# A one-core decoder layer with 64 streamed experts: two extra 1 MB weight slots, TensorE bodies written out, and one weight scaling and the closing norm reordered

## What is computed

```
scores = sigmoid(t @ router_w)                     # 256 tokens, 64 experts
...                                                # top 6 experts of the top 4 groups, gates w
a = einsum('td,edf->tef', t, w1)                   # w1, w3: 64 x 1024 x 256
b = einsum('td,edf->tef', t, w3)
hid = silu(a) * b * gates
routed = einsum('tef,efd->td', hid, w2)            # w2: 64 x 256 x 1024
shared = (silu(t @ sw1) * (t @ sw3)) @ sw2
x = x + gate_f * (routed + shared)
return rms_norm(x, final_norm_g)
```

## Time and profile before

| | us |
|---|---|
| median of 3 runs | 787.99 (787.81 to 791.71) |
| the profiled execution | 788.67 |
| its span, first to last instruction | 786.9 |
| PE busy, share of the span | 729.7, 93% |
| DVE busy | 325.1, 41% |
| ACT busy | 173.5, 22% |
| POOL busy | 8.6, 1% |
| moved by DMA | 271.33 MB, mean 345 GB/s |

### The profile page before, as it was taken

How to read it: one execution, slowest core, us unless ns; L and a number is a source line. 1 busy time by engine, 2 the same in 40 slices (tenths; PEclk the granted TensorE clock), 3 DMA queues, 4 the chain that set the end, 5 groups by cost and what they waited for, 6 DMA issues and landing times.

```text
span 786.9 us, 12545 instructions
## 1 busy us (share of the span) xinstructions
PE 729.7 (93%) x5000; PEld 389.4 (49%) x5000; DVE 325.1 (41%) x810; ACT 173.5 (22%) x348; POOL 8.6 (1%) x22
## 2 busy tenths in 40 slices
PE   4699999999999998999998998999999997999894
PEld 1478888888886454333343333343434332333332
DVE  1119493855556486323333233231333322323324
ACT  3223320200000232212122122120222211212213
POOL 0200001000000000000000000000000000000000
PEclk9999999999999998999999999999999999999997
DMA  9999627695959355999999999999999999999981
GB/s 338 378 348 365 195 88 221 234 310 182 349 203 418 143 237 211 370 421 421 420 420 421 420 421 420 421 421 419 384 421 420 421 418 420 422 419 421 421 354 53
DMA packets 73427, 271.33 MB, mean 345 GB/s; under 512 B 4424, under 2 KB 33232, under 8 KB 48416
## 3 DMA queue, kind: packets, MB, share of 16 engines
q1 hardware_dynamic: 71664, 264.26, 85.6%
q0 software_dynamic: 1408, 6.20, 2.2%
q10 hardware_dynamic: 304, 0.13, 0.1%
HBM read 269.51 MB, written 1.05 MB: 344 GB/s over the span
## 4 chain that ended last, share of the span: by engine, by line
PE 63%; DMA 24%; DVE 6%; SPq 3%; issue 2%; ACT 2%; DVEq 0%; ACTq 0%
PE bank L1092 62%; DMA ring<-exp_w_dram 21%; DMA ring<-ada_w_dram 2%; SPq L356 2%; SPq L359 1%; DVE slot_gate L1041 1%; PE bank L1407 1%; DVE reg L1045 1%; DVE reg L1036 1%; ACT reg L615 1%; DMA reg<-reg 1%; DVE h_hT L1083 0%; PE bank L1165 0%; DVE reg L937 0%; ACT L575 0%
## 5 line engine op out<-in xcount | busy, mean ns | idle before, releaser
L1092 PE MATMUL bank<-ring,h_hT 128*32 128x512 f32 (+2 forms) x2144 | 257.2, 590 | 19.6 <-DMA ring<-exp_w_dram 14.9
L1092 PEld LDWEIGHTS bank<-ring,h_hT 128*32 128x32 f32 (+1 forms) x2144 | 88.0, 114 | 179.7 <-issue 172.7
L1092 PE MATMUL bank<-h_hT,ring 128*128 128x256 f32 x704 | 155.4, 379 | 1.8 <-ACT h_hT L461 1.8
L1092 PEld LDWEIGHTS bank<-h_hT,ring 128*128 128x128 f32 x704 | 133.4, 190 | 20.5 <-ACT h_hT L461 2.0
L1092 PE MATMUL bank<-ring,turned 128*32 128x512 f32 x1024 | 118.8, 605 | 0.3
L1036 DVE TENSOR_TENSOR reg<-reg,bank 128x256 f32<-128x256 f32 x32 | 13.5, 421 | 196.7 <-ACT reg L615 196.7
L1059 DVE TENSOR_TENSOR bank<-bank,reg 128x512 f32<-128x512 f32 x64 | 44.8, 700 | 86.9 <-PE bank L1092 86.9
L1092 PEld LDWEIGHTS bank<-ring,turned 128*32 128x32 f32 x1024 | 30.6, 111 | 64.9 <-issue 61.3
L615 ACT ACTIVATE reg<-bank 128x256 f32<-128x256 f32 x32 | 12.3, 385 | 213.8 <-PE bank L1092 213.8
L1092 PE MATMUL bank<-take,h_part 128*128 128x256 f32 x288 | 51.4, 303 | 0.4 <-ACT h_hT L600 0.2
L1064 DVE TENSOR_TENSOR y_part<-bank,y_part 128x512 fp32r<-128x512 f32 x64 | 43.9, 686 | 2.4
(11 more groups left out here) (222 smaller groups left out, 432.3 us busy)
## 6 DMA issues: line engine op xcount, KB each, us to landing
ring<-exp_w_dram SPq DMA_DIRECT2D x192, 1024.0 KB, 15.9
ring<-ada_w_dram SPq DMA_DIRECT2D x24, 1024.0 KB, 12.6
ring<-w_in_dram SPq DMA_DIRECT2D x24, 1024.0 KB, 12.4
ring<-w_branch_dram SPq DMA_DIRECT2D x4, 1024.0 KB, 12.5
ring<-w_out_dram SPq DMA_DIRECT2D x4, 1024.0 KB, 8.1
ring<-shared_w_dram SPq DMA_DIRECT2D x2, 1024.0 KB, 13.7
reg<-ada_bp_dram POOLq DMA_DIRECT2D x3, 512.0 KB, 8.6
...
```

Of the source, the lines that this page charges most:

```text
L1092: return pe.matmul(o, lhsT, rhs, start=start, stop=stop, skip_group_check=True)
```

## The change

- Two more slots of 1 MB (`spare`) lie where the mixer half's buffers were; small buffers of that half (`par`, `crep` and others) move into the region that is given up, and `turned` takes the place of a constant that is no longer read, so that there is room. SP fills them with w1 and w3 of the first expert of the eighth pair (pair 7), between the w13 and the w2 transfers of pair 1, after waiting for the last reader and writer of the region (`acc_done`, `x2_done`, `x2_sq`). In the fourth loading step (`SPARE_PAIR // 2` = 3) half 1 then gets two w13 transfers in place of four. TensorE reads one expert of pair 7 from `spare`, the other from the ring.
- TensorE's bodies 0, 1 and 2 are written out. Only the last body is in a loop, whose count is read just ahead of it.
- DVE scales `shared_w2` between the first and the second body.
- In each pair DVE does product and subtraction of the first half, then of the second.
- The closing norm: DVE takes mean and variance of block 1 with its statistics instruction while ACT squares block 0 alone; block 1 is multiplied out and stored first.

```
@@ -54,6 +54,7 @@
+SPARE_PAIR = BODY_PAIRS - 1
...
-        turned = sb("turned", [P, 2, 2, P])
+        turned = const[:, C_AT["inv"]:C_AT["inv"] + 4 * P].rearrange("p (r j s) -> p r j s", r=2, j=2)
...
+        spare = sb("spare", [P, 2, UNIT])
...
-            def load_step(use, it):
+            def load_step(use, it, spared=False):
 
                 for r in range(RING_PAIRS):
                     sp.wait_ge(w13_used[r], use)
-                    for e in range(2):
+                    for e in range(spared and r == SPARE_PAIR % 2, 2):
                         for w in range(2):
                             load_13(r, e, w, it)
                     sp.wait_ge(w2_used[r], use)
@@ -381,10 +384,19 @@
                     for w in range(2):
                         sp.wait_ge(*used_up(LAST[6 * r + 2 * e + w]))
                         load_13(r, e, w, 0)
+                if r:
+                    sp.wait_ge(S["acc_done"], N_GATE)
+                    sp.wait_ge(S["x2_done"], 4)
+                    sp.wait_ge(S["x2_sq"], 4)
+                    for w in range(2):
+                        sp.dma_start(spare[:, w, :], w13_src[w][2 * SPARE_PAIR]).then_inc(spare_landed, 16)
                 for e in range(2):
                     sp.wait_ge(*used_up(LAST[6 * r + 4 + e]))
                     load_2(r, e, 0)
-            with sp.Fori(1, STEPS - 1) as it:
+            with sp.Fori(1, SPARE_PAIR // 2) as it:
+                load_step(it, it)
+            load_step(SPARE_PAIR // 2, SPARE_PAIR // 2, True)
+            with sp.Fori(SPARE_PAIR // 2 + 1, STEPS - 1) as it:
                 load_step(it, it)
...
-            for tb in range(TB):
-                for hf in range(2):
-                    act.wait_ge(S["sum_done"], hf + 1)
-                    act.activation(h2[:, tb, hf * 512:(hf + 1) * 512], bank[B_OUT[2 * tb + hf]][:, :], ACT.Square, scale=1.0 / 32,
-                                   accum_out=ssq[:, 2 * tb + hf:2 * tb + hf + 1]).then_inc(S["x3_sq"], 1)
-                act.wait_ge(S["x3_var"], tb + 1)
+            for hf in range(2):
+                act.wait_ge(S["sum_done"], hf + 1)
+                act.activation(h2[:, 0, hf * 512:(hf + 1) * 512], bank[B_OUT[hf]][:, :], ACT.Square, scale=1.0 / 32,
+                               accum_out=ssq[:, hf:hf + 1]).then_inc(S["x3_sq"], 1)
+            for tb in (1, 0):
+                act.wait_ge(S["x3_var"], 2 - tb)
                 act.activation(rstd[:, 10 + tb:11 + tb], rstd[:, 8 + tb:9 + tb], ACT.Sqrt).then_inc(S["x3_rstd"], 1)
...
                         dve.tensor_tensor(bank[B_Y[hf]][:, :], bank[B_Y[hf]][:, :], gate_f[:, hf * 512:(hf + 1) * 512], ALU.mult)\
                            .then_inc(S["y_gated"], 1)
-                    for hf in range(2):
                         cols = slice(hf * 512, (hf + 1) * 512)
                         dve.wait_ge(S["y_top"], 2 * n + (hf + 1))
                         dve.tensor_tensor(y_part[1][:, cols], bank[B_Y[hf]][:, :], y_part[0][:, cols], ALU.subtract)\
                            .then_inc(S["y_split"], 1)
 
-            with dve.Fori(0, SPLIT) as use:
+            with dve.Fori(0, 1) as use:
+                body(use)
+            dve.wait_ge(S["cast_read"], 8)
+            dve.wait_ge(S["sw2_in"], 16)
+            for j in range(2):
+                dve.tensor_tensor(shared_w2[:, j * D:(j + 1) * D], shared_w2[:, j * D:(j + 1) * D], gate_f, ALU.mult)\
+                   .then_inc(S["sw2_gated"], 1)
+            with dve.Fori(1, SPLIT) as use:
                 body(use)
...
-            for tb in range(TB):
-                dve.wait_ge(S["x3_sq"], 2 * tb + 2)
-                link(dve.tensor_scalar(rstd[:, 8 + tb:9 + tb], ssq[:, 2 * tb:1 + 2 * tb], ssq[:, 1 + 2 * tb:2 + 2 * tb], EPS,
-                                       ALU.add, ALU.add))
-                dve.reciprocal(rstd[:, 8 + tb:9 + tb], rstd[:, 8 + tb:9 + tb]).then_inc(S["x3_var"], 1)
-                dve.wait_ge(S["x3_rstd"], tb + 1)
+            for hf in range(2):
+                dve.wait_ge(S["sum_done"], hf + 1)
+                link(dve.bn_stats(stats[:, hf, :], bank[B_OUT[2 + hf]][:, :]))
+            link(dve.bn_aggr(mv[:, 0, :], stats[:, :, :]))
+            link(dve.scalar_tensor_tensor(out=rstd[:, 9:10], in0=mv[:, 0, 0:1], scalar=mv[:, 0, 0:1], in1=mv[:, 0, 1:2],
+                                          op0=ALU.mult, op1=ALU.add))
+            link(dve.tensor_scalar(rstd[:, 9:10], rstd[:, 9:10], EPS, None, ALU.add))
+            dve.reciprocal(rstd[:, 9:10], rstd[:, 9:10]).then_inc(S["x3_var"], 1)
+            dve.wait_ge(S["x3_sq"], 2)
+            link(dve.tensor_scalar(rstd[:, 8:9], ssq[:, 0:1], ssq[:, 1:2], EPS, ALU.add, ALU.add))
+            dve.reciprocal(rstd[:, 8:9], rstd[:, 8:9]).then_inc(S["x3_var"], 1)
+            for tb in (1, 0):
+                dve.wait_ge(S["x3_rstd"], 2 - tb)
...
-                    pe.wait_ge(w13_landed[r], (step + 1) * 64)
+                    spared = isinstance(use, int) and n == SPARE_PAIR
+                    late = r == SPARE_PAIR % 2 and not (isinstance(use, int) and n < SPARE_PAIR)
+                    if spared:
+                        pe.wait_ge(spare_landed, 32)
+                    pe.wait_ge(w13_landed[r], step * 64 + (32 if late else 64))
...
+                            w_k = spare_w[:, :, k, :] if spared and q % 2 == 0 else w13[:, q % 2, :, k, :]
                             ins = mm(bank[B_HID][side, :].rearrange("p (w f) -> p w f", w=2),
-                                     gathered_at(parity, gm, k)[:, side], w13[:, q % 2, :, k, :], k == 0, k == KD - 1)
+                                     gathered_at(parity, gm, k)[:, side], w_k, k == 0, k == KD - 1)
...
-            body(0)
-            with pe.Fori(1, SPLIT) as use:
+            spare_w = spare[:, :, :].rearrange("p w (k f) -> p w k f", k=KD)
+            for use in range(SPLIT):
                 body(use)
...
+            for use in range(SPLIT, BODIES - 1):
+                body(use)
             passes = pe.value_load(n_pass[0:1, 0:1], min_val=1, max_val=MAX_PASS)
-            with pe.Fori(SPLIT, passes * BODIES) as use:
+            with pe.Fori(BODIES - 1, passes * BODIES) as use:
                 body(use)
```

34 lines of the change are left out of this document (15 added, 19 removed).

## The result

The changed kernel takes 783.15 us (median of 7 runs, 780.64 to 785.04). The kernel before, in the runs of the same comparison and those shown above together, takes 790.25 us (median of 7, 787.81 to 791.71). The ratio is 0.9918, 95% interval 0.9896 to 0.994: 0.8% faster. The profiled execution of the changed kernel took 783.98 us, with a span of 782.1 us.

What follows compares the result with a forecast made beforehand. DMA transfers bound the loop (14.9 us a pair, TensorE 13.6). Spare slots 4.98 + scaling 2.35 + written-out bodies 0.6 - halves' order 0.36 = 7.6 us off the 787.99 median, 780.4 us; range 777.0 to 783.5.

Steps and rivals of the forecast that it cites:

- From one execution to the median: Whole kernel: the profiled execution is 0.68 us above the median, so 7.6 us comes off 787.99, giving 780.4.
- the fall of the clock in pair 0: Pair 0's second layer: 5.92 us against pair 1's 3.64; with a shorter idle time the clock should stay at 2.4 GHz.
- the scaling: Moving shared_w2's scaling behind pair 0: TensorE gains 3.94 us, the transfers 2.35, which is the value taken; bounds 1.5 and 3.94.
- the pace of the transfers: Loop: a load counts when its last DMA engine is done, so 1.3 us come and go; extra room in the range.
- the halves' order: Last pair: the second product comes 0.36 us later and everything behind it too; nothing hides it there.
- The spare slots: Two slots filled ahead of the loop take 2 MB out of its stream: 4.98 us gained, bounds 2 and 4.98.
- Rival (3): Spare slots buy less: TensorE becomes the limit before pair 15; at most the start's gain is left, 785.4 us; chance 0.05.
- Rival (1): The clock falls in pair 0 all the same: 0.85 us less gain, 781.3 us; chance 0.16.
- The bodies written out: Jump ahead of pair 24: TensorE's 4.5 us there are off the path; 0.6 us gained, bounds 0 and 1.3.
- rival (2): TensorE's whole 4.5 us at the jump ahead of pair 24 come off: 3.9 more, 776.5 us; chance 0.03.
- Rival (4): Bodies 1 and 2: written-out code doesn't reach TensorE in time, 24 us slower, about 804 us; chance 0.03.
- The norm: Closing norm behind the last scatter: 4.7 to 5.2 us against 4.92, so 0 gain; bounds -0.2 and +0.3.

Runs made afterwards that it cites:

- e5: The kernel before, unchanged, profiled once more: 788.27 us (one run).
- e7: The changed kernel without the spare slots, plus 32 loads of 8 KB in the loop, each a single row on one DMA engine: 789.35 us (one run).
- e8: The changed kernel without the spare slots, plus 32 loads of 8 KB, each as 16 rows of 512 B over all DMA engines: 789.24 us (one run).
- e12: The changed kernel with only the old order of the two halves put back, new norm kept: 782.12 us, ratio to before 0.9916.
- e1: The changed kernel without the two spare slots, pair 7 loaded through the ring like any other: 788.33 us, ratio to before 0.9981.
- e14: The changed kernel with the halves' old order, run a second time for comparison: 782.61 us, ratio to before 0.9928.
- e2: The changed kernel with the scaling of shared_w2 put back ahead of DVE's first body: 783.76 us, ratio to before 0.9918.
- e4: The changed kernel with both the old order of the halves and the old closing norm: 783.32 us, ratio to before 0.9912.
- e6: The kernel before with only the scaling of shared_w2 moved between DVE's bodies: 789.29 us, ratio to before 0.9998.
- e3: The changed kernel with TensorE's bodies in the two loops of before, one jump back ahead of pair 24: 782.85 us, ratio to before 0.9897.
- e11: The changed kernel, unchanged, run once more: 783.4 us, ratio to before 0.992.
- e13_warm_gaps: The changed kernel with the halves' old order and eight useless 256-column matmuls in TensorE's idle stretches ahead of the mixer: 780.92 us, ratio to before 0.9901.
- e10_warm_split: The changed kernel with the halves' old order, useless matmuls in TensorE's pauses and the residual's products moved into pair 12: 785.28 us, ratio to before 0.9951.

## Why the forecast was right, and where it was not

**From one execution to the median** is the step that failed: "The profiled execution is 0.68 above the median, so against the median: 787.99 - 7.6 = 780.4". It takes the clock of one profiled execution for that of all. Two things hang on it. What stands ahead of pair 0 was put at nothing, without a reason, and the fall of the clock in pair 0, on which most of the scaling's 2.35 us rest, was counted as if every execution had it. The runs show in its place that pair 0 starts anywhere from 300.60 to 304.26 us, in the changed kernel's profile 2.49 later than before, and that the scaling gives 0.9 us where the clock stays up. With that the sum is 5.05 + 0.9 + 0.16 - 0.17 = 5.9, as between the medians of all runs (5.9). That it fits so well is luck, for the medians are good to about a microsecond. It was luck too that the measured median lies in the range: the room that holds it was made for the pace of the transfers.

**The start of the loop**, by the traces:

```
1.2 GHz between 25 and 39 us   kernels                                     pair 0 at
none                           before, e5, e7, e8, e12                     300.60 to 300.83
3.4 us                         e1, e14                                     302.46, 302.81
6.8 us                         after, e2, e4, e6                           303.18 to 303.39
10.2 us                        e3, e11                                     304.20, 304.26
```

The table orders every trace but those with useless matmuls, whatever the layout of the buffers: e7 and e8 have the changed one and start early, e6 has the old one and starts late. e12_old_halves and e14_old_halves_again are one kernel, and it falls on either side. e13_warm_gaps shows that the clock decides it: where it is held up on purpose, all four runs are short. Why it falls in one execution and not in the next stays open. The two traces of the kernel before have no fall ahead of 40 us, but its timed runs point to some: of the 59 those with a mean clock of 0.983 or 0.984 took 789.0 to 792.6 us, those with 0.992 or 0.993 took 786.5 to 790.0. The traces' 0.988 is 19 us at 1.2 GHz and 0.983 is 27, so such runs have some 8 us more of it, though where isn't told. So a median of three of these runs is loose by 2 us, and a profiled execution that starts early has been set against a median of all sorts. Like is compared with like in e12_old_halves: with the early start it took 780.16 us in its profiled execution, 8.5 under the 788.67 of before, of which the halves' order has 0.24.

**The spare slots**: 4.98 forecast, 5.05 by the traces and 5.0 by the timed ratios. All of the reasons held: the free bytes at 284 us, no later transfer, no gap at pair 7, and TensorE not the limit up to pair 15, since it first waits for a transfer at pair 11, as forecast. The row of the changed kernel's timeline:

```profile
454.90 7.07 PE L1112 MATMUL bank<-ring,h_hT 128*32 128x512 f32 x64 [1.03 <-DMA ring<-exp_w_dram]
```

Rival (3) falls with it.

**The scaling**: 2.35 forecast for the transfers and 3.94 for TensorE; measured 2.36 and 3.87, between traces of before with the clock's fall and traces with the moved scaling without it. The mechanism and its sum were right for such an execution. But the forecast took the fall as a property of the kernel before, and e2_scale_first, idle for 2.55 us with the clock up, shows that it is one of some executions; there the move gives 0.9. Timed, all that is not the spare slots (e1_no_spare to before) is worth 0.19%, 1.5 us (0 to 3.0), where the forecast had 2.6, and the scaling alone none (e6_scale_only, up to 1.8). So this term was too high for a median by one to two. How often the clock falls in pair 0 of the kernel before I cannot tell: both its traces have it, and both are ones whose clock stayed up before 40 us, while e2_scale_first had fallen there. Some of its runs seem to have done without. The 6.8 us of this fall, 3.4 at the jump and the last 8.5 to 8.8 us make the 0.988 of its traces, and eleven of the 59 timed runs have 0.990 or more, which by this estimate leaves no room for 6.8 us; their median is 787.9 us, that of the others 789.3. Rival (1), the fall in pair 0 in spite of the shorter pause, is there too, once in thirteen traces with the moved scaling (e10_warm_split), at a price of 1.7 us for TensorE up to pair 1.

**The bodies written out**: 0.6 forecast, bounds 0 and 1.3; measured 0.1 to 0.2. The reading of the chain was right, the stall is off the path and rival (2) falls. What was wrong is to count the three pairs' 1.3 us of excess partly to the jump: without a jump, in e1_no_spare, the first layers of pairs 24 to 27 span 45.9 us, nearly the 46.05 of before. The Trainium skill, "Runtime: NRT & Kernel Launch", section "Instruction fetch mechanics", has a taken branch stall the engine where its target has to be fetched first, and says that kernels prefer full unrolling; the traces show the stall each time (3.78 us before, 3.69 in e3_loops) and that it is worth next to nothing here, since TensorE waits for transfers behind it. Rival (4), written-out code that doesn't arrive in time, shows nowhere: the pairs of the changed kernel run at 13.7 us up to pair 10 and then at the transfers' pace, 14.9.

**The end**: 0.36 later forecast for the halves' order, measured 0.17 against before (2.42 and 2.25) and 0.24 by the edit alone. The norm was put at 0, and it is 0 at the end. What stands behind the last first layer was to be 0.2 to 0.7 longer, and it is 24.95 against 25.22, shorter. This is the scatter, 1.44 and 1.77 us long, and 1.2 to 2.1 over all traces: it goes with the moment at which the clock falls in it. Between traces with a scatter of 1.2 us it is 24.76 in e6_scale_only, with the end of before, and 24.92 in e11_after_again and e3_loops: 0.16 longer.

By the traces, and with the clock's fall in pair 0, the terms add up to 5.05 + 2.36 + 0.16 - 0.17 = 7.4 of the 7.6.
